# The PEER gate table from one f32r product a token, with GpSimd making the weights' low parts

## The chip, the cores and the metric

The kernel runs on one core of one Trainium2 chip. The metric is the device time of one execution in microseconds (us); the lower, the better. The time before is 3590.15 us, the median of 3 runs (3589.37 to 3594.89).

Engines are named as in the profile: PE (TensorE, with PEld for its weight loads), ACT (ScalarE), DVE (VectorE), POOL (GpSimd), SP (the queue that issues the input DMAs).

## The reference, cut to what matters

The model is two transformer blocks on 512 tokens of width 1024. The part at hand is the PEER layer of the first block. It retrieves, for each token, 8 heads x 16 of 128 x 128 = 16384 single-neuron experts, and sums them with gates:

```python
top_s, pos = lax.top_k(cand, PEER_TOPK)
ids = jnp.take_along_axis(cand_id, pos, axis=-1)      # row * 128 + column
gate = jax.nn.softmax(top_s, axis=-1)
act = jax.nn.gelu(jnp.einsum('ted,td->te', u_emb[ids], xb))
out = jnp.einsum('te,ted->td', gate * act, v_emb[ids])
```

## The kernel before, in words

All matrix products with float32 accuracy are made of float32r parts: a weight tile is split into a high part (a copy rounded to f32r, made by ACT) and a low part (tile minus high part), and three products of 512 columns replace one. The PEER layer (`phase_peer`) computes all 16384 experts for all 512 tokens densely, and multiplies by a gate table that is zero nearly everywhere.

**Hidden units.** For each of 128 row groups n of 128 experts, `hidden` (L457) makes 24 matmuls of 512 columns (8 chunks of the width, three parts each; L463), ACT applies Gelu (`gelu`, L538) and writes the result to DRAM (`spill`, L543). `hi` (L443, ACT) and `lo` (L447) split the weight tile first. The tiles come through a ring of 4 slots, and the two parts lie in 2 slots each, so that `hi(n)` waits for `hidden(n-2)` to be done (semaphore `tiles_used`). The 128 steps are staged as `AHEAD` = 32 (`lo` on POOL, while DVE works out the top-k), `SPREAD` = 64 (the table stage) and `REST` = 32.

**The gate table.** In the table stage each step n also handles two batches m = 2n and 2n+1 of `GT` = 4 tokens. The row, column and gate of a token's 128 chosen experts lie on the 128 partitions (`rowT`, `colT`, `gateT`). A token's 128 x 128 table is the product of two one-hot matrices in float32: `cols` (iota equal to the column) as the weights, and `rows` (iota equal to the row, times the gate) as the moving side. `outers` (L467, matmuls at L477) makes 4 such products a batch into one PSUM bank of the four banks 4 to 7. `evac` (L562, ACT) copies a bank into the table in SBUF, transposed so that a token's entries lie 128 bytes apart, and `save` writes 32 tokens' table to DRAM.

**Who makes the one-hots.** `rows` always by DVE (`hots`, L776, one TENSOR_SCALAR of 128x128 a token). `cols` by POOL for even batches (`offset` L645 subtracts, `equal` L650 compares with 0), by ACT for m % 4 == 1 (`columns`: 4 times Abs at L550, one Relu of 1-x at L553), by DVE for m % 4 == 3 (L779). There are 8 batch buffers (`GR` = 8). `lo` is on DVE.

**What sets the order.** Each engine has its own program, a fixed list with semaphore waits, written by hand. One step of the table stage before:

```python
PE:   hidden(n); outers(2n); outers(2n+1)
ACT:  hi(n+1); gelu(n); spill(n-1); evac(2n); evac(2n+1); columns(2n+9) in every second step
DVE:  hots(2n); hots(2n+1); lo(n+1)
POOL: offset and equal, for the even batches
```

The loops have bodies of 8 steps; a loop's body is compiled once, and ACT's body holds two table loads (`ACT_TABLE_LOAD`), one at its first activation and one at its first Gelu.

After the 128 steps `mix` multiplies the hidden units, weighted by the table, with the second expert matrix. The second block follows. These parts are not touched.

Of the kernel before, what the change touches and what calls it, by code (L numbers as in the profile page):

```python
# [410 lines left out]
def phase_peer(nc, e, nxt, x, wt, val, idx, idxf, k, tb, mb):  # L411
# [9 lines left out]
    hot, hot_pool, hot_act = e.sem("hot"), e.sem("hot_pool"), e.sem("hot_act")  # L421
# [17 lines left out]
    def hi(act, it, step, n):  # L439

        act.wait_ge(e.slot_full[ring(n)], it * (4 * step) + 16 * ((base + n) // SLOTS + 1))
        act.wait_ge(e.tiles_used, it * step + (base + n + 3))
        A_(uh[:, slot(n)], e.ring[:, ring(n), 0:D], ACT.Copy).then_inc(e.hi_done, 1)  # L443

    def lo(eng, ops, it, step, n):
        eng.wait_ge(e.hi_done, it * step + (base + n + 1))
        ops.tensor_tensor(ul[:, slot(n)], e.ring[:, ring(n), 0:D], uh[:, slot(n)].bitcast(F32),  # L447
                          ALU.subtract).then_inc(e.lo_done, 1)

    def sp_program(sp):  # L450
        stream(e, sp, name, nxt)

    def pe_program(pe):
# [12 lines left out]

        def outers(it, m):  # L467

            r = m % GR
            pe.wait_ge(hot, it * 16 + (m + 1))  # L470
            if r % 2 == 0:
                pe.wait_ge(hot_pool, it * 8 + (m // 2 + 1))
            if r % 4 == 1:
                pe.wait_ge(hot_act, it * 4 + (m // 4 + 1))
            pe.wait_ge(stored, it * 16 + (m + 1))
            for t in range(GT):
                mm = M(e.ps[:, 4 + m % 4, t * P:(t + 1) * P], tb.cols[:, r, t], tb.rows[:, r, t])  # L477
            mm.then_inc(outer, 1)

        def mix(it, g, first, last):  # L480

            pe.wait_ge(e.lo_done, it * 8 + (base + NK + g + 1))
            pe.wait_ge(ready, it * 8 + (g + 1))
            for o in order:
                if first and o == 4:

                    pe.wait_ge(stored, batches + 4)
# [39 lines left out]
    def act_program(act):  # L527
        for s in range(SLOTS):
            act.sem_inc(spilled[s], 16)
        for s in range(2):  # L530
            act.sem_inc(saved[s], 16)
        act.sem_inc(stored, 4)
# [22 lines left out]
        def evac(it, m):  # L555

            blk = m // BK
            if m % BK == 0:
                act.wait_ge(saved[blk], it * 16 + 16)
            act.wait_ge(outer, it * 16 + (m + GR + 1))  # L560
            t0 = (m % BK) * GT
            A_(tb.table[:, blk].rearrange("p i t -> p t i")[:, t0:t0 + GT, :],  # L562
               e.ps[:, 4 + m % 4, :].rearrange("p (t i) -> p t i", t=GT), ACT.Copy).then_inc(stored, 1)

        def save(it, blk):

            act.wait_ge(stored, it * 16 + (BK * (blk + 1) + 4))
# [17 lines left out]
        for n in range(nb):  # L585
            act.wait_ge(turned, n + 1)
            for j, y in enumerate((e.rowT, e.colT, e.gateT)):
                cp = A_(y[:, n * P:(n + 1) * P], e.ps[:, 4 + n, j * P:(j + 1) * P], ACT.Copy)
            cp.then_inc(spread, 1)

        act.wait_ge(spread, nb)
        columns(0, 1)
        columns(0, 5)

        def table_step(it, n, more):
            hi(act, it, 8, AHEAD + n + 1)
            gelu(it, 8, AHEAD + n)
            spill(it, 8, AHEAD + n - 1)
            evac(it, 2 * n)
            evac(it, 2 * n + 1)  # L600
            if n % 2 == 0 and more:
                columns(it, 2 * n + 1 + GR)
            if n % 4 == 3:
                save(it, n // 4)

# [1 line left out]
            for n in range(8):  # L607
                table_step(it, n, True)
        for n in range(8):
            table_step(SPREAD // 8 - 1, n, n < 4)  # L610
        with act.Fori(0, REST // 4) as it:
            for n in range(AHEAD + SPREAD, AHEAD + SPREAD + 4):
                hi(act, it, 4, n + 1)
                gelu(it, 4, n)
                spill(it, 4, n - 1)
        spill(0, 4, NK - 1)

        def round_w(it, g):
# [13 lines left out]
    def pool_program(pool):  # L632
# [2 lines left out]
            for n in range(4):  # L635
                lo(pool, nc.gpsimd, it, 4, n)

        def offset(it, j):

            pool.wait_ge(outer, it * GR + (2 * j + 1))  # L640
            if not isinstance(it, int) or j:

                pool.wait_ge(pool_offset, it * (GR // 2) + j)
            col = it * (GR * GT) + 2 * j * GT
            nc.gpsimd.tensor_tensor(tb.cols[:, 2 * j % GR], c["iota"].unsqueeze(1).broadcast_to([P, GT, P]),  # L645
                                    e.colT[:, bass.ds(col, GT)].unsqueeze(2).broadcast_to([P, GT, P]),
                                    ALU.subtract).then_inc(pool_offset, 1)
# [5 lines left out]
        turns = batches // GR  # L653
        pool.wait_ge(spread, nb)
        offset(0, 0)
        with pool.Fori(0, turns - 1) as it:
            for j in range(GR // 2):
                offset(it, j + 1)
                equal(j)
        for j in range(GR // 2 - 1):  # L660
            offset(turns - 1, j + 1)
            equal(j)
        pool.wait_ge(pool_offset, GR // 2 * turns)
        equal(GR // 2 - 1)
# [28 lines left out]
    def dve_program(dve):  # L693
# [75 lines left out]

        def hots(it, m):  # L770

            r = m % GR
            dve.wait_ge(outer, it * 16 + (m + 1))
            for t in range(GT):
                col = it * (16 * GT) + (m * GT + t)
                oh = V.tensor_scalar(tb.rows[:, r, t], c["iota"], e.rowT[:, bass.ds(col, 1)],  # L776
                                     e.gateT[:, bass.ds(col, 1)], ALU.is_equal, ALU.mult)
                if r % 4 == 3:
                    oh = V.tensor_scalar(tb.cols[:, r, t], c["iota"], e.colT[:, bass.ds(col, 1)], None,  # L779
                                         ALU.is_equal)  # L780
            oh.then_inc(hot, 1)

        dve.wait_ge(e.lo_done, base + AHEAD)
        lo(dve, V, 0, 8, AHEAD)
        dve.wait_ge(spread, nb)
        with dve.Fori(0, SPREAD // 8) as it:
            for n in range(8):
                hots(it, 2 * n)
                hots(it, 2 * n + 1)
                lo(dve, V, it, 8, AHEAD + n + 1)  # L790
        with dve.Fori(0, REST // 4) as it:
            for n in range(AHEAD + SPREAD, AHEAD + SPREAD + 4):
                lo(dve, V, it, 4, n + 1)

        def weigh(it, g):
            q = g // GQ
# [1979 lines left out]
def hybrid_kernel(nc, w, out, stop=None):  # L2776
    with ExitStack() as ctx:
# [56 lines left out]
        with ExitStack() as outer:  # L2834
# [41 lines left out]
            tb.rows, tb.cols = a.take(GR, GT, P), a.take(GR, GT, P)  # L2876
# [162 lines left out]
```

## Time and profile before

| | |
|---|---|
| median of 3 runs | 3590.15 us (3589.37 to 3594.89) |
| the profiled execution: own time, span | 3598.26 us, 3596.5 us |
| PE busy, share of the span | 3509.6 us, 98% |
| DVE, ACT, POOL busy | 1772.6, 1283.5, 500.7 us |
| table stage, first to last table matmul | 699.8 to 1164.8 us |
| mean granted clock of TensorE | 0.985 |

The profile comes from one execution; "busy" is the time in which an engine executes instructions, with waits, register work and DMA issue left out. A matmul's duration overlaps that of the next, so that its cost is the distance from start to start. A float32 matmul shows as two records. A start on POOL or ACT just behind its releaser shows how long a semaphore takes. An engine's idle time matters only where that engine is waited for.

### The profile page before, as it was taken

The page shows a single profiled execution, that of the slowest core. Times are in us where ns is not written, and L with a number is a line of the kernel's source. Part 1 is how long each engine was busy: PE and PEld are TensorE (multiplying, and loading weights), DVE is VectorE, ACT ScalarE, POOL GpSimd, SP SyncE. Part 2 cuts the span into 40 slices and gives each one's busy share as a digit, 9 for nine tenths or more (in the row PEclk, how much of TensorE's full clock was granted, in tenths as well). Part 3 has the DMA queues.
Part 4 walks back from the last instruction along what each step waited for, and adds up shares of the span by engine and source line. Part 5 has one row for each costly group of instructions (what it writes and reads, how often), then busy time and mean ns, then how long its engine had stood idle before and what let it go on. Part 6 is the DMA issues. An engine that isn't in the chain of part 4 may idle for free. (4 is left out here: it accounts for less than half of the span.)

```text
span 3596.5 us, 52641 instructions
## 1 busy us (share of the span) xinstructions
PE 3509.6 (98%) x19484; PEld 2990.6 (83%) x19484; DVE 1772.6 (49%) x3403; ACT 1283.5 (36%) x1851; POOL 500.7 (14%) x428
## 2 busy tenths in 40 slices
PE   8999999999999999999999999999999999899999
PEld 8966787788888878888888899998889789768887
DVE  7344599566665224444444543335445456654333
ACT  4244222466665232222222322233223333333232
POOL 0100125433332001111111010010100000111011
PEclk9989999999999999999999999999999989999999
DMA  4200224355555546666666422222222100122221
GB/s 148 77 18 18 88 95 140 123 175 175 178 181 184 190 144 190 194 189 193 190 193 197 129 88 94 82 94 74 91 85 77 59 1 1 36 76 97 93 99 69
DMA packets 115447, 416.05 MB, mean 116 GB/s; under 512 B 14192, under 2 KB 14320, under 8 KB 113008
## 3 DMA queue, kind: packets, MB, share of 16 engines
q1 hardware_dynamic: 75632, 279.93, 23.6%
q0 software_dynamic: 18944, 67.12, 6.4%
q10 hardware_dynamic: 20736, 67.12, 5.0%
q8 instruction: 95, 1.56, 0.2%
q14 instruction: 40, 0.33, 0.0%
HBM read 344.91 MB, written 69.21 MB: 115 GB/s over the span
## 5 line engine op out<-in xcount | busy, mean ns | idle before, releaser
L447 DVE TENSOR_TENSOR w_lo<-ring,w_hi 128x1024 fp32r<-128x1024 f32 x224 | 275.4, 1230 | 698.0 <-ACT w_hi L443 698.0
L183 DVE TENSOR_TENSOR w_lo<-ring,w_hi 128x1024 fp32r<-128x1024 f32 (+2 forms) x157 | 205.9, 1311 | 568.7 <-ACT w_hi L177 568.7
L443 ACT ACTIVATE w_hi<-ring 128x1024 fp32r<-128x1024 f32 x255 | 270.2, 1059 | 505.9 <-PE ps L493 488.8
L463 PE MATMUL ps<-hn_hi,w_hi 128*128 128x512 f32 x1024 | 408.1, 398 | 3.6 <-POOL w_lo L447 1.4
L463 PE MATMUL ps<-hn_lo,w_hi 128*128 128x512 f32 x1024 | 404.5, 395 | 0.0
L463 PE MATMUL ps<-hn_hi,w_lo 128*128 128x512 f32 x1024 | 402.9, 393 | 0.0
L493 PE MATMUL ps<-units_hi,w_hi 128*128 128x512 f32 x1024 | 399.1, 390 | 2.7 <-DVE units_lo L804 2.7
L493 PE MATMUL ps<-units_hi,w_lo 128*128 128x512 f32 x1024 | 399.0, 390 | 0.0
L493 PE MATMUL ps<-units_lo,w_hi 128*128 128x512 f32 x1024 | 398.9, 390 | 0.0
L177 ACT ACTIVATE w_hi<-ring 128x1024 fp32r<-128x1024 f32 (+2 forms) x170 | 190.2, 1119 | 455.0 <-PE ps L241 381.0
L241 PE MATMUL ps<-f_hn_hi,w_hi 128*128 128x264 f32 (+1 forms) x1056 | 284.6, 324 | 8.9 <-DVE f_hn_lo L855 8.5
L241 PE MATMUL ps<-f_hn_lo,w_hi 128*128 128x264 f32 (+1 forms) x1056 | 284.9, 324 | 0.0
L241 PE MATMUL ps<-f_hn_hi,w_lo 128*128 128x264 f32 (+1 forms) x1056 | 283.7, 323 | 0.0
L463 PEld LDWEIGHTS ps<-hn_hi,w_hi 128*128 128x128 f32 x1024 | 192.8, 188 | 48.8 <-ACT scratch L538 4.2
L463 PEld LDWEIGHTS ps<-hn_hi,w_lo 128*128 128x128 f32 x1024 | 192.6, 188 | 43.5
L493 PEld LDWEIGHTS ps<-units_hi,w_hi 128*128 128x128 f32 x1024 | 192.6, 188 | 43.1 <-issue 3.1
L463 PEld LDWEIGHTS ps<-hn_lo,w_hi 128*128 128x128 f32 x1024 | 192.5, 188 | 42.1
L493 PEld LDWEIGHTS ps<-units_lo,w_hi 128*128 128x128 f32 x1024 | 192.6, 188 | 40.1
L493 PEld LDWEIGHTS ps<-units_hi,w_lo 128*128 128x128 f32 x1024 | 192.5, 188 | 40.1
L241 PE MATMUL ps<-hn_hi,mix_w_hi 128*128 128x264 f32 (+1 forms) x752 | 211.8, 332 | 6.0 <-DVE hn_lo L855 4.1
L538 ACT ACTIVATE scratch<-ps 128x512 f32<-128x512 f32 x128 | 76.6, 598 | 375.7 <-PE ps L463 375.6
L241 PE MATMUL ps<-hn_lo,mix_w_hi 128*128 128x264 f32 (+1 forms) x752 | 209.6, 329 | 0.0
(432 smaller groups left out, 6723.6 us busy)
## 6 DMA issues: line engine op xcount, KB each, us to landing
ring<-in_w_uv SPq DMA_DIRECT2D x256, 512.0 KB, 3.4
ring<-in_f_up SPq DMA_DIRECT2D x88, 512.0 KB, 3.2
expert_units<-scratch ACTq DMA_DIRECT2D x128, 256.0 KB, 2.6
gate_table<-peer ACTq DMA_DIRECT2D x16, 2048.0 KB, 7.2
peer<-gate_table POOLq DMA_DIRECT2D x32, 1024.0 KB, 8.0
peer<-expert_units POOLq DMA_DIRECT2D x128, 256.0 KB, 3.7
ring<-in_w_in SPq DMA_DIRECT2D x29, 512.0 KB, 3.3
ring<-in_w_late SPq DMA_DIRECT2D x25, 512.0 KB, 3.3
```

The lines of the kernel that those rows point to most:

```text
L177: self.nc.scalar.activation(self.h[:, self.slot(k), 0:self.cols], e.ring[:, self.ring(k), 0:self.cols], ACT.Copy).then_inc(e.hi_done, 1)
L183: self.nc.vector.tensor_tensor(self.l[:, self.slot(k), 0:self.cols], e.ring[:, self.ring(k), 0:self.cols], self.h[:, self.slot(k), 0:self. ...
L241: mm = nc.tensor.matmul(e.ps[:, bank + hf, 0:tokens.width], lhsT[:, wt.slot(k), col], rhs(part, c)[:, cut], start=(c == 0 and j == 0), sto ...
L443: A_(uh[:, slot(n)], e.ring[:, ring(n), 0:D], ACT.Copy).then_inc(e.hi_done, 1)
L447: ops.tensor_tensor(ul[:, slot(n)], e.ring[:, ring(n), 0:D], uh[:, slot(n)].bitcast(F32), ALU.subtract).then_inc(e.lo_done, 1)
L463: mm = M(e.ps[:, n % 2, :], u[:, slot(n), ch * P:(ch + 1) * P], x[part][:, ch, META:L], start=(ch == 0 and j == 0), stop=(ch == DC - 1 and ...
L493: mm = M(e.ps[:, o, :], v[:, slot(NK + g), col], w[:, g % 2], start=(first and j == 0), stop=(last and j == 2))
L538: A_(units[:, n % SLOTS, 0:T], e.ps[:, n % 2, :], ACT.Gelu).then_inc(gelu_done, 1)
```

## The change

- **PE** (`outers`): one float32r matmul a token with 256 columns takes the place of the float32 matmul with 128 columns. The moving side `rows` holds the high part of the gate and the low part beside it ([2, 128] a token); a batch takes two PSUM banks, and two batches are in flight (`stored` starts at 2) where four were.
- **ACT**: `evac` goes; `high` (L558) copies the high half of a batch from PSUM to SBUF. `columns` now makes all the one-hot columns: for every batch one Abs (L551) and one Relu (L553) over 512 elements, in place, on differences that POOL made. `hi` is made two steps ahead and comes after `gelu`.
- **DVE**: `hots` makes a token's rows by one SCALAR_TENSOR_TENSOR of 128x256 (L773); `evac` (L787) adds the low half in PSUM to the copied high half and writes the table. `lo` leaves DVE in the table stage.
- **POOL** (`table_step`): `lo`, then two `offset` (L643); `equal` goes.

The core of the diff:

```diff
@@ PE @@
         def outers(it, m):
-            r = m % GR
             pe.wait_ge(hot, it * 16 + (m + 1))
-            if r % 2 == 0:
-                pe.wait_ge(hot_pool, it * 8 + (m // 2 + 1))
-            if r % 4 == 1:
-                pe.wait_ge(hot_act, it * 4 + (m // 4 + 1))
+            pe.wait_ge(hot_col, it * 16 + (m + 1))
             pe.wait_ge(stored, it * 16 + (m + 1))
             for t in range(GT):
-                mm = M(e.ps[:, 4 + m % 4, t * P:(t + 1) * P], tb.cols[:, r, t], tb.rows[:, r, t])
+                mm = M(both(m)[:, t].rearrange("p x i -> p (x i)"), tb.cols[:, m % GR, t],
+                       tb.rows[:, m % 4, t].rearrange("p x i -> p (x i)"))
@@ ACT @@
         def columns(it, m):
-            act.wait_ge(outer, it * 16 + (m + 1))
-            for t in range(GT):
-                col = it * (16 * GT) + (m * GT + t)
-                off = A_(tb.cols[:, m % GR, t], c["iota"], ACT.Abs, bias=e.colT[:, bass.ds(col, 1)], scale=-1.0)
-            off.then_inc(act_offset, 1)
-            act.wait_ge(act_offset, it * 4 + (m // 4 + 1))
-            A_(tb.cols[:, m % GR], tb.cols[:, m % GR], ACT.Relu, bias=e.one, scale=-1.0).then_inc(hot_act, 1)
+            x = tb.cols[:, m % GR]
+            act.wait_ge(pool_offset, it * 16 + (m + 1))
+            A_(x, x.bitcast(F32), ACT.Abs).then_inc(act_offset, 1)
+            act.wait_ge(act_offset, it * 16 + (m + 1))
+            A_(x, x.bitcast(F32), ACT.Relu, bias=e.one, scale=-1.0).then_inc(hot_col, 1)
+        def high(it, m):
+            act.wait_ge(outer, it * 16 + (m + GR + 1))
+            A_(tb.high[m % 2], both(m)[:, :, 0], ACT.Copy).then_inc(copied, 1)
         def table_step(it, n, more):
-            hi(act, it, 8, AHEAD + n + 1)
+            if more:
+                columns(it, 2 * n + 4)
+                columns(it, 2 * n + 5)
             gelu(it, 8, AHEAD + n)
             spill(it, 8, AHEAD + n - 1)
-            evac(it, 2 * n)
-            evac(it, 2 * n + 1)
-            if n % 2 == 0 and more:
-                columns(it, 2 * n + 1 + GR)
+            hi(act, it, 8, AHEAD + n + 2)
+            high(it, 2 * n)
+            high(it, 2 * n + 1)
             if n % 4 == 3:
                 save(it, n // 4)
@@ POOL @@
+        def offset(it, m):
+            pool.wait_ge(outer, it * 16 + (m + 1))
+            nc.gpsimd.tensor_tensor(tb.cols[:, m % GR], c["iota"].unsqueeze(1).broadcast_to([P, GT, P]),
+                                    e.colT[:, bass.ds(it * (16 * GT) + m * GT, GT)].unsqueeze(2).broadcast_to([P, GT, P]),
                                     ALU.subtract).then_inc(pool_offset, 1)
-        def equal(j):
-            nc.gpsimd.tensor_scalar(tb.cols[:, 2 * j], tb.cols[:, 2 * j], 0.0, None,
-                                    ALU.is_equal).then_inc(hot_pool, 1)
+        def table_step(it, n, more):
+            lo(pool, nc.gpsimd, it, 8, AHEAD + n + 2)
+            if more:
+                offset(it, 2 * n + 6)
+                offset(it, 2 * n + 7)
         pool.wait_ge(spread, nb)
+        for m in range(6):
+            offset(0, m)
@@ DVE @@
         def hots(it, m):
-            dve.wait_ge(outer, it * 16 + (m + 1))
+            dve.wait_ge(outer, it * 16 + (m + GR - 4 + 1))
             for t in range(GT):
                 col = it * (16 * GT) + (m * GT + t)
-                oh = V.tensor_scalar(tb.rows[:, r, t], c["iota"], e.rowT[:, bass.ds(col, 1)],
-                                     e.gateT[:, bass.ds(col, 1)], ALU.is_equal, ALU.mult)
+                parts = tb.gates[:, bass.ds(col, 1)].bitcast(F32).rearrange("p o x -> p (o x)")
+                oh = V.scalar_tensor_tensor(out=tb.rows[:, m % 4, t],
+                                            in0=c["iota"].unsqueeze(1).broadcast_to([P, 2, P]),
+                                            scalar=e.rowT[:, bass.ds(col, 1)],
+                                            in1=parts.unsqueeze(2).broadcast_to([P, 2, P]),
+                                            op0=ALU.is_equal, op1=ALU.mult)
+        def evac(it, m):
+            dve.wait_ge(copied, it * 16 + (m + 1))
+            V.tensor_tensor(tb.table[:, blk].rearrange("p i t -> p t i")[:, t0:t0 + GT, :], tb.high[m % 2],
+                            both(m)[:, :, 1], ALU.add).then_inc(stored, 1)
+        def table_step(it, n, more):
+            if more:
+                hots(it, 2 * n + 2)
+                hots(it, 2 * n + 3)
+            evac(it, 2 * n)
+            evac(it, 2 * n + 1)
```

ACT, one step in the body of the table loop. `scratch<-ps` is Gelu's result, `peer` the region of one-hots and table. Before:

```order
L443 ACTIVATE w_hi<-ring 128x1024 [waits tiles_used,slot_full3]
L536 REGISTER_ALU
L538 ACTIVATE scratch<-ps 128x512 [waits spilled1,tiles_used]
L542 REGISTER_ALU
L543 ISA [waits gelu_done]
L543 DMA expert_units<-scratch 128x512
L560 REGISTER_ALU
L562 ACTIVATE peer<-ps 128x4x128 [waits outer]
```

With the change, from the first of a step's two `columns` (the same two rows again, and a second `high`, are left out):

```order
L551 ACTIVATE hot_cols<-hot_cols 128x512 [waits pool_offset]
L553 ACTIVATE hot_cols<-hot_cols,misc 128x512 [waits act_offset]
...
L540 ACTIVATE scratch<-ps 128x512 [waits spilled3,tiles_used]
...
L444 ACTIVATE w_hi<-ring 128x1024 [waits tiles_used,slot_full2]
L557 REGISTER_ALU
L558 ACTIVATE scratch<-ps 128x512 [waits outer]
```

The copy to `w_hi` stood ahead of Gelu and now stands behind it, and two pairs of activations that wait for POOL (`pool_offset`) stand ahead of Gelu.

POOL in the body of its table loop, before:

```order
L643 REGISTER_ALU [waits outer]
L645 ISA [waits pool_offset]
L645 TENSOR_TENSOR peer<-const_tab,turned 128x512
L650 TENSOR_SCALAR peer<-peer 128x512
L640 REGISTER_ALU
```

With the change, one step:

```order
L448 TENSOR_TENSOR w_lo<-ring,w_hi 128x1024 [waits hi_done]
L642 REGISTER_ALU
L643 ISA [waits outer]
L643 TENSOR_TENSOR hot_cols<-const_tab,turned 128x512
L642 REGISTER_ALU
L643 ISA [waits outer]
L643 TENSOR_TENSOR hot_cols<-const_tab,turned 128x512
```

The comparison is gone, the subtraction is there twice a step where it was there once, and the weights' low part, which waits for ACT's `hi_done`, stands ahead of both.

## Rows read from the trace of the kernel before

**Rows 1.** The page: span, and busy time of each engine.

```profile
span 3596.5 us, 52641 instructions
PE 3509.6 (98%) x19484; PEld 2990.6 (83%) x19484; DVE 1772.6 (49%) x3403; ACT 1283.5 (36%) x1851; POOL 500.7 (14%) x428
```

**Rows 2.** Windows, inside the table stage: busy of each engine, granted clock, DMA.

```profile
720.00:1135.00 415.00, 415.00 (x2265) 355.82 (x2264) 257.39 (x623) 267.80 (x380) 141.87 (x113) 1.00 0.51 177
```

**Rows 3.** Timeline of PE (start, duration), one table step; L477's records.

```profile
761.13 0.48 PE L463 MATMUL ps<-hn_hi,w_hi 128*128 128x512 f32 x1
...
766.77 1.95 PE L477 MATMUL ps<-peer 128*128 128x128 f32 x16
768.47 0.48 PE L463 MATMUL ps<-hn_hi,w_hi 128*128 128x512 f32 x1
...
L477 PE MATMUL ps<-peer x1024: 272/275/275, 699.8 to 1164.8; 128*128 128x128 f32 x171
```

**Rows 4.** Timeline of PE, float32r matmuls of 264 columns, full rate.

```profile
2100.12 0.41 PE L241 MATMUL ps<-f_hn_lo,w_hi 128*128 128x264 f32 x2
...
2109.68 0.41 PE L241 MATMUL ps<-f_hn_lo,w_hi 128*128 128x264 f32 x2
```

**Rows 5.** Timeline of ACT: Relu and its follower, Gelu and its follower; L562 min/median/max.

```profile
823.34 0.72 ACT L553 ACTIVATE peer<-peer,misc 128x512 f32<-128x512 f32 x1
823.97 1.04 ACT L443 ACTIVATE w_hi<-ring 128x1024 fp32r<-128x1024 f32 x1
...
1170.74 0.60 ACT L538 ACTIVATE scratch<-ps 128x512 f32<-128x512 f32 x1 [2.78 <-PE ps L463]
1171.43 1.06 ACT L443 ACTIVATE w_hi<-ring 128x1024 fp32r<-128x1024 f32 x1
...
L562 ACT ACTIVATE peer<-ps x128: 1082/1130/1226, 702.0 to 1165.1; 128x512 f32<-128x512 f32 x128
```

**Rows 6.** From ACT's high part to POOL's low part; POOL's durations at both lines.

```profile
648.53 1.06 ACT L443 ACTIVATE w_hi<-ring 128x1024 fp32r<-128x1024 f32 x1
...
649.67 3.13 POOL L447 TENSOR_TENSOR w_lo<-ring,w_hi 128x1024 fp32r<-128x1024 f32 x1 [3.48 <-ACT w_hi L443]
...
L447 POOL TENSOR_TENSOR w_lo<-ring,w_hi x32: 2384/2408/4379, 497.6 to 677.5; 128x1024 fp32r<-128x1024 f32 x32
...
L645 POOL TENSOR_TENSOR peer<-const_tab,turned x64: 1032/1044/1187, 693.9 to 1134.9; 128x512 f32<-128x512 f32 x64
```

**Rows 7.** Timeline of DVE and POOL where their two-input instructions meet.

```profile
534.24 2.29 DVE L752 TENSOR_TENSOR peer<-peer,const_tab 128x2048 f32<-128x2048 f32 x1
536.45 4.49 DVE L753 TENSOR_TENSOR peer<-peer,const_tab 128x2048 f32<-128x2048 f32 x1
...
534.77 4.01 POOL L447 TENSOR_TENSOR w_lo<-ring,w_hi 128x1024 fp32r<-128x1024 f32 x1 [3.31 <-ACT w_hi L443]
```

**Rows 8.** DVE: three kinds of instruction near the new ones.

```profile
532.65 0.29 DVE L741 SCALAR_TENSOR_TENSOR peer<-peer 128x128 f32<-128x128 f32 x1
532.86 0.28 DVE L743 TENSOR_TENSOR peer<-peer 128x128 f32<-128x128 f32 x1
...
L1507 DVE SCALAR_TENSOR_TENSOR scratch<-z,param_tab,scratch x12: 767/768/770, 2717.5 to 2793.6; 128x527 f32<-128x527 f32 x12
...
L1157 DVE TENSOR_TENSOR scratch<-ps,scratch x44: 681/696/708, 2070.7 to 3526.4; 128x528 f32<-128x528 f32 x22, 128x512 f32<-128x512 f32 x22
```

**Rows 9.** ACT's table loads at L443 and L538.

```profile
L443 ACT ACT_TABLE_LOAD x7: 1283/1283/1283, 697.8 to 1049.9; - x7
...
L538 ACT ACT_TABLE_LOAD x8: 1283/1283/1283, 504.0 to 1053.3; - x8
```

**Rows 10.** PE's gap, and windows (PE, PEld, DVE, ACT, POOL busy, PEclk, DMA).

```profile
2878.92 0.71 PE L2586 MATMUL ps<-gates,const_tab 16*128 16x128 f32 x4 [2.10 <-DVE delta L2675]
...
2880.00:2884.00 4.00, 2.81 (x16) 2.44 (x15) 1.54 (x6) 1.10 (x3) 0.00 (x0) 0.50 0.01 2
...
510.00:680.00 170.00, 167.33 (x719) 134.48 (x718) 142.96 (x392) 49.50 (x60) 85.08 (x30) 1.00 0.40 134
```

More of the change, by code:

```diff
@@ L420, in phase_peer @@
     expd, gated, turned, spread = (e.sem(n) for n in ("gates_exp", "gated", "gates_turned", "gates_spread"))
-    hot, hot_pool, hot_act = e.sem("hot"), e.sem("hot_pool"), e.sem("hot_act")
+    hot, hot_col = e.sem("hot"), e.sem("hot_col")
+    parted, copied = e.sem("gate_parts"), e.sem("high_copied")
     pool_offset, act_offset = e.sem("pool_offset"), e.sem("act_offset")
@@ L448, in lo, with both @@
                           ALU.subtract).then_inc(e.lo_done, 1)
+    def both(m):
+        at = (4 + 2 * (m % 2)) * WIDE
+        return e.psf[:, at:at + 2 * WIDE].rearrange("p (t x i) -> p t x i", t=GT, x=2)
     def sp_program(sp):
@@ L485, in mix @@
                 if first and o == 4:
-                    pe.wait_ge(stored, batches + 4)
+                    pe.wait_ge(stored, batches + 2)
                 if first and o == 0:
@@ L545, in columns @@
         def columns(it, m):
-            act.wait_ge(outer, it * 16 + (m + 1))
-            for t in range(GT):
-                col = it * (16 * GT) + (m * GT + t)
-                off = A_(tb.cols[:, m % GR, t], c["iota"], ACT.Abs, bias=e.colT[:, bass.ds(col, 1)], scale=-1.0)
-            off.then_inc(act_offset, 1)
-            act.wait_ge(act_offset, it * 4 + (m // 4 + 1))
-            A_(tb.cols[:, m % GR], tb.cols[:, m % GR], ACT.Relu, bias=e.one, scale=-1.0).then_inc(hot_act, 1)
[L555 to L559, printed above, removed]
+            x = tb.cols[:, m % GR]
[4 more added lines that the diff above has]
+        def high(it, m):
             act.wait_ge(outer, it * 16 + (m + GR + 1))
-            t0 = (m % BK) * GT
-            A_(tb.table[:, blk].rearrange("p i t -> p t i")[:, t0:t0 + GT, :],
-               e.ps[:, 4 + m % 4, :].rearrange("p (t i) -> p t i", t=GT), ACT.Copy).then_inc(stored, 1)
+            A_(tb.high[m % 2], both(m)[:, :, 0], ACT.Copy).then_inc(copied, 1)
         def save(it, blk):
-            act.wait_ge(stored, it * 16 + (BK * (blk + 1) + 4))
+            act.wait_ge(stored, it * 16 + (BK * (blk + 1) + 2))
             act.dma_start(e.gtab[it * 2 + blk],
@@ L587, in act_program @@
             for j, y in enumerate((e.rowT, e.colT, e.gateT)):
-                cp = A_(y[:, n * P:(n + 1) * P], e.ps[:, 4 + n, j * P:(j + 1) * P], ACT.Copy)
-            cp.then_inc(spread, 1)
+                A_(y[:, n * P:(n + 1) * P], e.ps[:, 4 + n, j * P:(j + 1) * P], ACT.Copy)
+            A_(tb.gates[:, n * P:(n + 1) * P, 0], e.ps[:, 4 + n, 2 * P:3 * P], ACT.Copy).then_inc(spread, 1)
         act.wait_ge(spread, nb)
-        columns(0, 1)
-        columns(0, 5)
+        hi(act, 0, 8, AHEAD + 1)
+        for m in range(4):
+            columns(0, m)
         def table_step(it, n, more):
-            hi(act, it, 8, AHEAD + n + 1)
+            if more:
+                columns(it, 2 * n + 4)
+                columns(it, 2 * n + 5)
             gelu(it, 8, AHEAD + n)
             spill(it, 8, AHEAD + n - 1)
-            evac(it, 2 * n)
-            evac(it, 2 * n + 1)
-            if n % 2 == 0 and more:
-                columns(it, 2 * n + 1 + GR)
+            hi(act, it, 8, AHEAD + n + 2)
+            high(it, 2 * n)
+            high(it, 2 * n + 1)
             if n % 4 == 3:
@@ L609, in act_program @@
         for n in range(8):
-            table_step(SPREAD // 8 - 1, n, n < 4)
-        with act.Fori(0, REST // 4) as it:
+            table_step(SPREAD // 8 - 1, n, n < 6)
+        with act.Fori(0, REST // 4 - 1) as it:
             for n in range(AHEAD + SPREAD, AHEAD + SPREAD + 4):
-                hi(act, it, 4, n + 1)
                 gelu(it, 4, n)
+                hi(act, it, 4, n + 2)
                 spill(it, 4, n - 1)
+        for n in range(NK - 4, NK):
+            gelu(0, 4, n)
+            if n < NK - 1:
+                hi(act, 0, 4, n + 2)
+            spill(0, 4, n - 1)
         spill(0, 4, NK - 1)
@@ L636, in pool_program @@
                 lo(pool, nc.gpsimd, it, 4, n)
[L638 to L646, printed above, removed]
-                                    ALU.subtract).then_inc(pool_offset, 1)
-        def equal(j):
-            nc.gpsimd.tensor_scalar(tb.cols[:, 2 * j], tb.cols[:, 2 * j], 0.0, None,
-                                    ALU.is_equal).then_inc(hot_pool, 1)
-        turns = batches // GR
-        pool.wait_ge(spread, nb)
[L655 to L664, printed above, removed]
+        def offset(it, m):
+            pool.wait_ge(outer, it * 16 + (m + 1))
+            nc.gpsimd.tensor_tensor(tb.cols[:, m % GR], c["iota"].unsqueeze(1).broadcast_to([P, GT, P]),
+                                    e.colT[:, bass.ds(it * (16 * GT) + m * GT, GT)].unsqueeze(2).broadcast_to([P, GT, P]),
+                                    ALU.subtract).then_inc(pool_offset, 1)
+        def table_step(it, n, more):
[3 more added lines that the diff above has]
+                offset(it, 2 * n + 7)
+        pool.wait_ge(spread, nb)
+        for m in range(6):
+            offset(0, m)
+        pool.wait_ge(e.lo_done, base + AHEAD + 2)
+        with pool.Fori(0, SPREAD // 8 - 1) as it:
+            for n in range(8):
+                table_step(it, n, True)
+        for n in range(8):
+            table_step(SPREAD // 8 - 1, n, n < 5)
         def load_gates(it, q):
@@ L783, in dve_program @@
         dve.wait_ge(e.lo_done, base + AHEAD)
         lo(dve, V, 0, 8, AHEAD)
+        lo(dve, V, 0, 8, AHEAD + 1)
+        dve.sem_inc(stored, 2)
         dve.wait_ge(spread, nb)
-        with dve.Fori(0, SPREAD // 8) as it:
-            for n in range(8):
[L788 to L791, printed above, removed]
+        V.tensor_tensor(tb.gates[:, :, 1], e.gateT, tb.gates[:, :, 0].bitcast(F32), ALU.subtract).then_inc(parted, 1)
@@ L792, in dve_program @@
+        dve.wait_ge(parted, 1)
+        hots(0, 0)
+        hots(0, 1)
+        with dve.Fori(0, SPREAD // 8 - 1) as it:
+            for n in range(8):
+                table_step(it, n, True)
+        for n in range(8):
+            table_step(SPREAD // 8 - 1, n, n < 7)
+        dve.wait_ge(e.lo_done, base + AHEAD + SPREAD + 2)
+        with dve.Fori(0, REST // 4 - 1) as it:
             for n in range(AHEAD + SPREAD, AHEAD + SPREAD + 4):
-                lo(dve, V, it, 4, n + 1)
+                lo(dve, V, it, 4, n + 2)
@@ L795, in weigh @@
+        for n in range(NK - 4, NK - 1):
+            lo(dve, V, 0, 4, n + 2)
         def weigh(it, g):
@@ L2875, in hybrid_kernel @@
             a, tb = Arena(region), Env()
-            tb.rows, tb.cols = a.take(GR, GT, P), a.take(GR, GT, P)
+            a.take(2 * GR * GT * P)
+            tb.rows = work.at("hot_rows", 0, GR // 2, GT, 2, P, dt=F32R)
+            tb.cols = work.at("hot_cols", 4 * GR * GT * P, GR, GT, P, dt=F32R)
+            tb.gates = work.at("gate_parts", room + 12 * T, T, 2, dt=F32R)
+            tb.high = [x[:, 0:GT * P].rearrange("p (t i) -> p t i", t=GT) for x in (e.r0, e.r1)]
             tb.table = a.take(2, NK, GB)
```

9 lines of the change are left out of this document (4 added, 5 removed).

## The prediction

> **What bounds the kernel now.** I read the page first: PE is busy for 3509.6 of 3596.5 us [rows 1], so time is won or lost only where PE's own work shrinks or where PE is made to wait. Then the windows: between 720 and 1135 us, deep in the table stage, PE is busy for all of the 415 us at full clock, while DVE works for 257, ACT for 268 and POOL for 142 us [rows 2]. So nobody holds PE there today. Then the timeline of PE for one step: 24 matmuls of 512 columns take from 761.13 to 766.77, which is 5.64 us, and the eight float32 table matmuls (16 records) from 766.77 to 768.47, 1.70 us, so a step takes 7.34 us [rows 3]. L477's first and last record, 699.8 and 1164.8, are 63 steps and 15 records of about 0.11 us apart, which gives 7.355 us a step on average [rows 3]. The stage has 64 steps. The AHEAD, REST and mix stages and the second block keep PE's work as it is.
>
> **What the change takes from PE.** A token's product becomes one float32r matmul of 256 columns. The nearest row is the 264-column float32r matmul with a weight load of its own: from 2100.12 to 2109.68 there are 13 rounds of six, 78 matmuls in 9.56 us, 0.123 us each [rows 4]. Eight take 0.98 us where 1.70 were. PE alone would then need 5.64 + 0.98 = 6.62 us a step, and 64 x 0.72 = 46 us would be won. It cannot be much more (256 columns are 3% fewer than 264) and not less than nothing (1.70 us, if 256 columns cost as much as the two float32 records).
>
> **What the change puts on the other engines.** The costs per step, with their rows:
> - ACT: the high part (start to start of what follows on POOL) 1.14 us [rows 6]; Gelu to its follower 0.69 us [rows 5]; Abs and Relu of 512 elements four times. Relu today takes 0.63 us to its follower [rows 5]; the new Abs has the same shape, and each Relu waits for the Abs before it by a semaphore, so I take 0.65 for all four, 2.60 us. Two `high` copies have Gelu's shape and source, 0.60 each; the 1.13 us of the scattered copy at L562 [rows 5] leave ACT. Together 5.6 us.
> - POOL: the low part 2.41 us when undisturbed, and two subtractions of 1.04 us each [rows 6], 4.49 us.
> - DVE: eight SCALAR_TENSOR_TENSOR of 256 elements. The same kind takes 0.29 us for 128 elements and 0.768 for 527 [rows 8], a slope of 1.2 ns, so 0.44 us for 256; start to start is 0.08 less (532.65 to 532.86 for a duration of 0.29 [rows 8]), and register pointers give some back: 0.40 us, eight times 3.2 us. The `evac` add with one operand from PSUM took 0.70 us for 512 to 528 elements written densely [rows 8]; its bounds are that and 1.23, since the scattered write cost ACT 0.53 us more than a dense one (1.13 against 0.60 [rows 5]). I take 1.2, as the same scatter is written; two are 2.4 us. Together 5.6 us.
>
> The Trainium skill warns, in "Vector Engine (DVE) Microarchitecture Reference", points that are easy to get wrong, that this instruction halves its throughput with two float32 inputs in SBUF. The row speaks against it (527 elements in 768 ns, two inputs in SBUF [rows 8]); by the rule a token's rows would cost 0.67 us and eight of them 5.4, and the sum would go up by what the access rival below has.
>
> Every engine alone fits into 6.62 us. But the fixed lists tie two of them into a **ring**. ACT makes hi(n+2) behind gelu(n); POOL's lo(n+2) waits for it; POOL makes offset(2n+6) and offset(2n+7) behind lo(n+2), in its own order; ACT's columns(2n+6) and columns(2n+7) wait for them, and they stand *ahead* of gelu(n+1) and so of hi(n+3), for which lo(n+3) waits. The stock of six offsets and four columns made before the loop is consumed without any step of slack, since the offsets that step n+1 needs are made in step n behind lo(n+2). One turn of the ring is one step:
>
> hi to POOL's start 1.14 + lo 2.41 + first offset 1.04 + signal to ACT 0.08 + two columns 2.60 + Gelu 0.69 = 7.96 us.
>
> The signal is from the same row pair (1.14 less 1.06 [rows 6]). The way round by the second offset is shorter: 1.14 + 2.41 + 2.08 + 0.08 + 1.30 + 0.69 = 7.70 us. The two `high` copies (1.20 us) lie beside lo and the first offset (3.45 us) and cost nothing; if they came late (an `outers` kept back by DVE), the ring would wait by as much. So the ring is longer than PE's 6.62, and longer than the 7.355 of now.
>
> **The shared access of DVE and POOL** comes on top. POOL's low part at 534.77 took 4.01 us instead of 2.41: it met DVE's L752, ran out only once that had ended at 536.5, and then L753, the same kind as L752, took 4.49 instead of 2.29 because it stood until POOL had ended at 538.8 [rows 7]. One instruction with two inputs in SBUF keeps out the other engine's for its whole length. A step now holds POOL's 4.49 and DVE's 3.2 us of such work, 7.7 us of a turn of 8. Bounds for what this adds to the ring: nothing, if DVE's eight fall into the stretch in which ACT has the ring (columns, Gelu, hi: 4.4 us); 0.40 for each of lo and the first offset, 0.8 us, if each meets a running DVE instruction. DVE's adds wait for `high`, which comes just behind the start of lo, so its eight mostly fall behind POOL's work; I take 0.14. A step then takes 8.10 us.
>
> **Table loads.** ACT's loop body has two loads of 1.28 us [rows 9], at its first activation and its first Gelu, once in 8 steps. Now PE covers them. In the ring they stand behind the wait for POOL and ahead of hi: 8 x 2 x 1.28 = 20 us (none to 20; for each to be hidden the ring must be waiting for another engine at that moment).
>
> **Entry of the stage.** ACT makes hi(33) and four columns ahead of its first Gelu, POOL makes six offsets ahead of lo(34), and DVE's rows share the access with these. PE's first table matmuls could start some us later than 699.8: 0 to 5 us, taken at 2. The `save` of every fourth step now waits for DVE's adds (2.4 us behind the first `high`, within the 3.45 us for which ACT waits for POOL anyway): nothing. REST: the low part is made earlier than now and PE does the same matmuls; nothing.
>
> **Sum.** 64 x (8.10 - 7.355) = 48, + 20 + 2 = +70 us. The profiled execution took 3598.26 us, so it would take 3668; the median shown lies 8 us lower, so 3660 us.
>
> **The rivals.**
> - *PE stays the bound* (the other side). If the ring turned in less than 6.62 us, the step would be PE's: -46 us, 3544 us. It decides at a turn of 7.355 us: below it the change wins. It needs 1.3 us less than the sum of measured durations, for instance if Abs and Relu on 512 elements took 0.3 us each. Rows 5 and 6 speak against it. Chance 0.11. A turn within 0.1 us of 7.355, no change, 0.03.
> - *The access becomes the bound.* If DVE's 3.9 us (0.49 each, with 0.05 more for the pointers than its duration) and POOL's 4.49 exclude each other and the adds (2.4) fall between them instead of beside POOL, a turn is up to 10.8 us; with partial overlap 9 to 10: 64 x 1.65 to 64 x 2.65 and the loads, +126 to +190 us, 3716 to 3780 us. For it speaks how little is free (0.4 us of 8.1); against it that ACT's share of the ring leaves DVE 4.4 us. Chance 0.13. In the Trainium skill, "SBUF — State Buffer", SBUF: two separate sides, only DVE instructions with two SBUF inputs or in a two-port mode take the shared pair, by which the adds, with one input in PSUM, would stay beside POOL; no row here shows it.
> - *PE's clock.* PE would idle 8.1 - 6.6 = 1.5 us a step, more at the loads. After a gap of 2.10 us at 2878.92 the granted clock was 0.50 for the next stretch, while 170 us with 2.7 us of gaps in all kept 1.00 [rows 10]. If each step's gap cost 4 us at half clock, 2 us of PE work are lost, PE needs 8.6 and with its gap 9 or more: +105 us and up, 3695 us. The gaps are shorter than the one that did it; chance 0.08.
> - *The change doesn't do what it says*: 256-column products as dear as before. PE would need 7.34, still below the ring: the result would be the forecast's. That is why the ring, not the product, decides.
>
> **The numbers.** The forecast's case has 0.65, with a range of its own from 3626 (ring at 7.75 by 0.2 us of overlap, half of the loads hidden) to 3700. The range to 8 in 10 goes from 3615 to 3745; it leaves out the faster and same cases (0.14) and the top of the access case. About 0.2% (7 us) is what a measurement of this kernel can tell from no change. Faster 0.11, same 0.03, slower 0.86.
>
> **What would show it.** Right: between PE's table matmuls and its next 512-column matmul a gap of about 1.5 us, ended by POOL's w_lo; ACT idle before Abs, ended by POOL; POOL idle before w_lo, ended by ACT; steps of 8 to 8.5 us; 256-column matmuls at 0.12 us. Wrong: PE busy all of the stage with steps of 6.6 us; or DVE without idle time; or the gaps ended by the one-hot rows or by the adds; or a granted clock well below 1.

## The result, and the profile after

The changed kernel takes 3631.51 us, the median of 4 runs (3630.99 to 3634.01), against 3592.22 us before (4 runs). The ratio is 1.0107 with a 95% interval of 1.0093 to 1.0121: **39 us slower**. The forecast was 3660 us, slower, with a range of 3615 to 3745. The direction was right and the time lies in the range, but 70 us were forecast where 39 came.

The page of the changed kernel, as [rows 1]:

```profile
span 3632.3 us, 51347 instructions
PE 3488.7 (96%) x18972; PEld 2943.7 (81%) x18972; DVE 1911.6 (53%) x3340; ACT 1315.6 (36%) x1951; POOL 642.8 (18%) x492
```

Windows over the same stretch of the table stage (busy of PE, PEld, DVE, ACT and POOL, granted clock, DMA), as [rows 2]:

```profile
720.00:1135.00 415.00, 366.90 (x1649) 289.47 (x1649) 343.94 (x515) 272.87 (x423) 245.64 (x156) 0.97 0.45 164
```

PE is no longer busy all of the time: 48 of 415 us are lost. Its products' line says what PE waited for there, as [rows 3] (durations min/median/max in ns, first and last start; then idle us and times; the idle lines also count the products' weight loads on PEld, to which `issue` belongs, and PE by itself waited for L787 for 55.1 us and for L773 for 1.9):

```profile
L479 PE MATMUL ps<-hot_rows,hot_cols x512: 276/283/554, 697.4 to 1202.4; 128*128 128x256 f32 x171
...
  issue: 87.5, 110
  DVE peer L787: 55.1, 103
  DVE hot_rows L773: 4.4, 4
```

From the first to the last product it takes 505.0 us, where it took 465.0 [rows 3]: +40.0 us. From PE's first matmul of the layer to the first product it is 2.9 us longer. Together that is a little more than the difference of the medians. (In the profiled executions the changed kernel was 5.3 us shorter before the layer and 1.8 us shorter behind the last product, where both kernels do the same, so that the spans are only 35.8 us apart. All comparisons of the stage below go from the first to the last product.)

One turn of the ring in the changed kernel, from the timelines of ACT, POOL and DVE (start, duration, idle before and what ended it):

```profile
804.84 1.05 ACT L444 ACTIVATE w_hi<-ring 128x1024 fp32r<-128x1024 f32 x1
805.79 1.07 ACT L558 ACTIVATE scratch<-ps 128x512 f32<-128x512 f32 x2
809.68 0.63 ACT L551 ACTIVATE hot_cols<-hot_cols 128x512 fp32r<-128x512 f32 x1 [2.82 <-POOL hot_cols L643]
810.34 0.72 ACT L553 ACTIVATE hot_cols<-hot_cols,misc 128x512 fp32r<-128x512 f32 x1
810.97 0.61 ACT L551 ACTIVATE hot_cols<-hot_cols 128x512 fp32r<-128x512 f32 x1
811.62 0.72 ACT L553 ACTIVATE hot_cols<-hot_cols,misc 128x512 fp32r<-128x512 f32 x1
812.25 0.58 ACT L540 ACTIVATE scratch<-ps 128x512 f32<-128x512 f32 x1
812.73 1.05 ACT L444 ACTIVATE w_hi<-ring 128x1024 fp32r<-128x1024 f32 x1
...
805.97 2.40 POOL L448 TENSOR_TENSOR w_lo<-ring,w_hi 128x1024 fp32r<-128x1024 f32 x1 [3.03 <-ACT w_hi L444]
808.33 2.49 POOL L643 TENSOR_TENSOR hot_cols<-const_tab,turned 128x512 fp32r<-128x512 f32 x2
...
806.41 2.03 DVE L787 TENSOR_TENSOR peer<-scratch,ps 128x512 f32<-128x512 f32 x2 [0.81 <-ACT scratch L558]
808.29 4.80 DVE L773 SCALAR_TENSOR_TENSOR hot_rows<-const_tab,turned,gate_parts 128x256 fp32r<-128x256 f32 x8
```

There is no idle time in it that one of the two engines does not owe to the other: hi 804.84, 1.13 to the low part at 805.97, 2.36 to the subtraction at 808.33, 1.35 to Abs at 809.68, 2.57 for the two columns, 0.48 from Gelu at 812.25 to the next hi at 812.73. The turn is 7.89 us. DVE's eight rows, which start with POOL's subtractions, take 4.80 us.

Where the body of ACT's loop ends and begins, the turn has the two table loads in it:

```profile
820.58 1.04 ACT L444 ACTIVATE w_hi<-ring 128x1024 fp32r<-128x1024 f32 x1
...
825.10 1.28 ACT L551 ACT_TABLE_LOAD   x1 [2.50 <-DVE peer L787]
...
829.08 1.28 ACT L540 ACT_TABLE_LOAD   x1
...
830.86 1.05 ACT L444 ACTIVATE w_hi<-ring 128x1024 fp32r<-128x1024 f32 x1
```

This one is 10.28 us. A body of 8 steps takes 64.8 us by the starts of `hi` (7.6 to 7.9 for seven steps, 10.3 for one) where it took 58.7.

### The profile page after: what moved, and what is told of

The parts are those of the page before. It is cut to its first block and busy times, and to the rows that moved or that the text cites. A ratio compares the mean times of both kernels' runs of the same rounds, so it can differ in the third digit from the quotient of the medians.

```text
span 3632.3 us, 51347 instructions
## 1 busy us (share of the span) xinstructions
PE 3488.7 (96%) x18972; PEld 2943.7 (81%) x18972; DVE 1911.6 (53%) x3340; ACT 1315.6 (36%) x1951; POOL 642.8 (18%) x492
## 5 line engine op out<-in xcount | busy, mean ns | idle before, releaser
L448 DVE TENSOR_TENSOR w_lo<-ring,w_hi 128x1024 fp32r<-128x1024 f32 x160 | 197.0, 1231 | 518.5 <-ACT w_hi L444 518.5
L448 POOL TENSOR_TENSOR w_lo<-ring,w_hi 128x1024 fp32r<-128x1024 f32 x96 | 243.2, 2534 | 393.6 <-ACT w_hi L444 303.3
L773 DVE SCALAR_TENSOR_TENSOR hot_rows<-const_tab,turned,gate_parts 128x256 fp32r<-128x256 f32 x512 | 308.1, 669 | 0.0
```

What stands on the lines that cost most here:

```text
L773: oh = V.scalar_tensor_tensor(out=tb.rows[:, m % 4, t], in0=c["iota"].unsqueeze(1).broadcast_to([P, 2, P]), scalar=e.rowT[:, bass.ds(col, 1)],
```

## The experiments

All edits are to the changed kernel. The stage column is the time from the first to the last product in each run's trace (before 465.0, changed kernel 505.0).

| run | median us | ratio to before, 95% | stage us |
|---|---|---|---|
| e1_pool_order | 3636.55 | 1.0127 (1.0101 to 1.0154) | 507.2 |
| e2_act_order | 3630.05 | 1.0108 (1.0085 to 1.0131) | 498.1 |
| e3_half_rows | 3632.89 | 1.0114 (1.0093 to 1.0135) | 505.3 |
| e4_twice_products | 3627.60 | 1.0092 (1.0073 to 1.0112) | 502.2 |
| e5_flat_act | 3625.04 | 1.0078 (1.0054 to 1.0103) | 491.2 |
| e6_pool_order_half_rows | 3555.12 | 0.9896 (0.9879 to 0.9913) | 427.8 |
| e7_gates_in_psum | 3624.86 | 1.0092 (1.0075 to 1.0108) | 496.2 |
| e8_psum_act_order | 3541.26 | 0.9856 (0.9839 to 0.9872) | 412.3 |
| e9_psum_pool_order | 3552.15 | 0.9890 (0.9873 to 0.9906) | 422.4 |
| e10_psum_both_orders | 3542.47 | 0.9856 (0.9834 to 0.9879) | 412.4 |
| e11_e8_twice_products | 3601.47 | 1.0025 (1.0012 to 1.0038) | 473.3 |

### Opening the ring: e1 and e2

```diff
@@ POOL, table_step @@
-            lo(pool, nc.gpsimd, it, 8, AHEAD + n + 2)
             if more:
                 offset(it, 2 * n + 6)
                 offset(it, 2 * n + 7)
+            lo(pool, nc.gpsimd, it, 8, AHEAD + n + 2)
```

> GpSimd's two subtractions of a step stand ahead of its low part instead of behind it; nothing else changes. The ring theory (ACT's hi, POOL's lo, POOL's offset, ACT's columns, Gelu, hi, one turn a step, 7.85 us by the changed kernel's profile): the columns no longer wait for lo, one turn now serves two steps, and the step falls to what comes next, PE's 6.6 or DVE's 6.9 us, 3560 to 3580 us. The access theory (POOL's 4.5 and DVE's 3.2 us of two-input instructions exclude each other, 7.7 us a step): the step stays at 7.6 to 7.8 us, 3610 to 3632 us. The buffer theory (PE waits for the adds because only two batches fit into PSUM): no change, 3631 us.

```diff
@@ ACT, table_step @@
-            if more:
-                columns(it, 2 * n + 4)
-                columns(it, 2 * n + 5)
             gelu(it, 8, AHEAD + n)
             spill(it, 8, AHEAD + n - 1)
             hi(act, it, 8, AHEAD + n + 2)
             high(it, 2 * n)
             high(it, 2 * n + 1)
+            if more:
+                columns(it, 2 * n + 4)
+                columns(it, 2 * n + 5)
```

> ACT makes the columns of batches 2n+4 and 2n+5 at the end of step n, behind the two high copies, instead of at its start, ahead of Gelu; nothing else changes. Ring theory: the differences that a step needs are then a whole step old, the ring is open as in e1_pool_order, 3560 to 3580 us. Access theory: as in e1, 3610 to 3632 us. Buffer theory: no change.

Neither won anything that the intervals show: 3636.55 and 3630.05 us. e2 falls into the range of the access theory; e1 lies above every range that was given. Taken by themselves the two times speak against the ring. But the ring is open in both: between 720 and 1135 us ACT waited for POOL's subtractions for 124.5 us in the changed kernel, and not once in e1 or e2. And the steps are not those of the changed kernel. By the starts of `hi`, e1's body from 769.4 us has steps of 4.97, 5.73, 11.18, 7.63, 5.47, 6.44, 10.61 and 11.28 us, no longer seven equal ones. Windows of e1 and of e2 (columns as above):

```profile
720.00:1135.00 415.00, 366.72 (x1630) 295.86 (x1629) 384.72 (x508) 275.74 (x420) 250.36 (x153) 0.93 0.45 162
```

```profile
720.00:1135.00 415.00, 373.75 (x1671) 301.72 (x1670) 410.74 (x527) 276.63 (x423) 264.68 (x157) 0.94 0.44 164
```

DVE is now busy for 385 and 411 of 415 us, with the same work as before. The timeline of e2 shows with what (DVE first, then POOL):

```profile
767.91 8.64 DVE L773 SCALAR_TENSOR_TENSOR hot_rows<-const_tab,turned,gate_parts 128x256 fp32r<-128x256 f32 x8
...
786.16 3.22 DVE L773 SCALAR_TENSOR_TENSOR hot_rows<-const_tab,turned,gate_parts 128x256 fp32r<-128x256 f32 x8
```

```profile
768.17 2.40 POOL L643 TENSOR_TENSOR hot_cols<-const_tab,turned 128x512 fp32r<-128x512 f32 x2
770.92 2.59 POOL L448 TENSOR_TENSOR w_lo<-ring,w_hi 128x1024 fp32r<-128x1024 f32 x1 [0.35 <-ACT w_hi L444]
773.48 2.40 POOL L643 TENSOR_TENSOR hot_cols<-const_tab,turned 128x512 fp32r<-128x512 f32 x2
```

The eight rows take 3.22 us where POOL does not hold them up and 8.64 us where POOL works nearly without a break: DVE stands for POOL's instructions, and "busy" counts that. So the ring was opened, and the shared access of DVE and POOL took its place at about the same length. In part this is still an inference here, since PE's granted clock fell too (0.93 and 0.94), and ACT's Gelu waits for PE in both runs (57 and 80 us of the window). As an estimate from these rows, the clock can explain at most 0.07 x 415 = 29 us and 0.06 x 415 = 25 us of the window. e7 and e8 below take away the access itself.

### Less work for one engine: e3 and e4

```diff
@@ DVE, hots @@
-            for t in range(GT):
+            for t in range(GT // 2):
@@ PE, outers @@
-                       tb.rows[:, m % 4, t].rearrange("p x i -> p (x i)"))
+                       tb.rows[:, m % 4, t % 2].rearrange("p x i -> p (x i)"))
```

> Leaves out DVE's rows of every batch's third and fourth token; their products use the rows of the first two. DVE does 1.6 us less a step, all of it on the access shared with POOL. Ring theory: POOL's offset loses only its 0.14 us of waiting, so 64 x 0.1 to 0.2 us, 3618 to 3626 us. Access theory: 7.7 less 1.6 is under PE's 6.6, so the step is PE's: 3555 to 3570 us.

It took 3632.89 us with a stage of 505.3: the 1.6 us a step that DVE no longer works are worth nothing. DVE is busy for 263.59 us of the window instead of 343.94, and POOL's subtractions are as long as before (1224 ns on average against 1225). This is the mirror of e1 and e2: with the access relieved, the ring holds the step alone. The gain of 0.1 to 0.2 us a step that was expected did not come, since the four rows that are left of a step's eight still meet POOL's subtractions.

```diff
@@ PE, outers @@
-            for t in range(GT):
+            for t in [t for t in range(GT) for _ in range(2)]:
```

> Each of the table's products is computed twice in a row (same result); PE does 8 matmuls of about 0.12 us more a step, 0.98 us. Ring theory: PE idles 1.1 us a step, and the copies wait for the products for 0.5 us more a batch, for which ACT has time while POOL works: 0 to 15 us more, 3631 to 3646 us. Were PE, or the way products, copy, add, products the bound: 63 us more, 3694 us.

It took 3627.60 us, 502.2 for the stage: PE's additional work is free in the changed kernel. The time is even 3 us below the range that was expected. In this run more of the steps last 7.6 us instead of 7.9, and POOL's subtractions take 1180 ns on average instead of 1225; why they meet DVE less was not tested.

### Both at once: e6

e6 has the edits of e1 and of e3.

> e1_pool_order and e3_half_rows together: the subtractions ahead of the low part, and the rows of every batch's third and fourth token left out. Each alone changed nothing. Two bounds in parallel (the ring at 7.85 us and the shared access at 7.7 to 8.0 us a step, each hiding the other): with both gone the step is PE's 6.5 to 6.6 us, 64 x 1.3 us less, 3540 to 3560 us. Another bound (PSUM's two batches, the copies, the adds): no change, 3615 to 3635 us.

It took 3555.12 us, 76 us less than the changed kernel, although each edit alone gave nothing. Two bounds of nearly the same length lay side by side, and each hid the other. That the second one is the access, and not DVE's own amount of work, is not shown by this pair, which takes both away; e7 to e9 leave DVE all of its work.

### What the two engines share: e7

```diff
@@ DVE @@
-                parts = tb.gates[:, bass.ds(col, 1)].bitcast(F32).rearrange("p o x -> p (o x)")
+                parts = e.psf[:, bass.ds(2 * WIDE + 2 * col, 2)]
...
         dve.wait_ge(parted, 1)
+        V.tensor_copy(e.psf[:, 2 * WIDE:4 * WIDE],
+                      tb.gates.bitcast(F32).rearrange("p t x -> p (t x)")).then_inc(parted, 1)
+        dve.wait_ge(parted, 2)
```

> DVE's rows read the gates' two parts from PSUM (banks 2 and 3, free in this stage, filled once by a copy of 1024 columns) instead of SBUF; all is computed. If what shuts DVE and POOL out of one another is two inputs in SBUF, a step's eight rows take 3.3 us instead of 4.8, and POOL's subtractions 1.04 instead of 1.2. The ring still turns in 7.7: 3615 to 3628 us. If DVE's rows still meet POOL: no change in either.

Groups of instructions between 715 and 1120 us, the changed kernel first, then e7 (count, then busy us and mean ns of one):

```profile
L773 DVE SCALAR_TENSOR_TENSOR hot_rows<-const_tab,turned,gate_parts 128x256 fp32r<-128x256 f32 x403 | 243.1, 671 | 0.0
L643 POOL TENSOR_TENSOR hot_cols<-const_tab,turned 128x512 fp32r<-128x512 f32 x101 | 121.9, 1225 | 0.0
```

```profile
L773 DVE SCALAR_TENSOR_TENSOR hot_rows<-const_tab,turned,ps 128x256 fp32r<-128x256 f32 x411 | 164.4, 477 | 0.0
L643 POOL TENSOR_TENSOR hot_cols<-const_tab,turned 128x512 fp32r<-128x512 f32 x103 | 105.3, 1045 | 0.0
```

With one of the two inputs in PSUM the rows no longer wait for POOL: 477 ns instead of 671, and POOL's subtraction is back at 1045 [rows 6]. What kept the two apart is thus shown to be DVE's pair of SBUF inputs. The stage is 8.8 us shorter (496.2; median 3624.86, 7 us less): every turn of the ring is now 7.6 us, but for the one in 8 with the table loads (10.3).

### Both at once, with all of the work: e8, e9, e10

e8 has the edits of e7 and e2, e9 those of e7 and e1, e10 all three.

> e7_gates_in_psum and e2_act_order together, all computed: the ring open and the shared access free. Two bounds in parallel: PE's 6.5 to 6.6 us a step, table loads covered by PE, 3545 to 3565 us, below the kernel before. If only the ring or only the access counted, one of e2 and e7 would have shown it alone: then 3615 to 3630 us here too.

> e7_gates_in_psum and e1_pool_order together, all computed: the same two bounds taken away, the ring by the other engine's order. ACT's columns still stand ahead of Gelu, whose wait for PE then sets them late: 3545 to 3575 us by the theory of two parallel bounds; else 3615 to 3635 us.

> e8_psum_act_order with GpSimd's subtractions ahead of its low part as well. If the ring was open already in e8, the low part now comes 2 us later and nothing is won: 3540 to 3550 us.

e8 takes 3541.26 us, ratio 0.9856: 51 us *below* the kernel before, 90 below the changed kernel. It computes everything that they do. The time is 4 us below the range that was expected. Its window, and PE's timeline at a step's end:

```profile
720.00:1135.00 415.00, 415.00 (x2026) 347.36 (x2025) 313.01 (x598) 317.48 (x491) 267.76 (x183) 1.00 0.58 206
```

```profile
853.86 0.39 PE L469 MATMUL ps<-hn_hi,w_lo 128*128 128x512 f32 x1
854.09 1.11 PE L479 MATMUL ps<-hot_rows,hot_cols 128*128 128x256 f32 x8
855.03 0.40 PE L469 MATMUL ps<-hn_hi,w_hi 128*128 128x512 f32 x1
```

PE is busy for all of the window at full clock (the table stage ends inside it, at 1109). Eight products take 0.94 us from start to start of their neighbours, and a step 6.51 us. e9 has 10.39 us for one step in 8, where the columns with their table load stand ahead of Gelu and a `save` waits for DVE's adds; e8 has the columns at the step's end, and that step is 7.7 us, followed by one of 5.4. By the starts of `hi`, a body takes 53.6 us in e9 and 52.1 in e8, which over six bodies is 9 of the 10 us between the two. e10 adds nothing to e8, as expected.

### The product's price: e11, and the table loads: e5

> e8_psum_act_order with each table product computed twice (same result), 8 matmuls of 0.12 us more a step. PE being the bound of e8, 64 x 0.92 to 0.98 us more: 3600 to 3604 us; in the changed kernel the same edit cost nothing (e4). It gives the price of a product where PE is the bound.

e11 (e8 with e4's edit) takes 60.2 us more than e8, 61.0 in the stage: 0.95 us a step. The same edit cost the changed kernel nothing. So a float32r product costs what PE's timeline says, once PE is the bound.

```diff
@@ ACT @@
-        with act.Fori(0, SPREAD // 8 - 1) as it:
+        for it in range(SPREAD // 8 - 1):
```

> The changed kernel with ACT's table loop written out (7 bodies of 8 steps without a loop), so that the two table loads and the branch of each body go; the order of everything is kept. Ring theory: the long steps of 10.3 us become 7.85, 7 x 2.4 = 17 us less, 3612 to 3617 us; if the shared access is as tight a bound as the ring, it gives part of that back, 3615 to 3628 us. Loads hidden: 3631 us.

The stage fell by 13.8 us, to 491.2. A body of 8 steps takes 62.6 us instead of 64.8, with no step above 7.9. The median fell by 6 us only, and its four runs lie between 3617.91 and 3628.24; in the profiled one, 7 of the 13.8 us are lost again behind the layer, where the kernels do the same. I take the stage's number for the loads; where the 7 us went stays open.

## Why the prediction was right or wrong

**Right: the other side's argument.** PE alone would have won 46 us. e8 won 51 against before, and e11 priced the eight products at 0.95 us, where the 264-column row [rows 4] gave 0.98.

**Right: the ring.** Its place, its members and its direction were those of the trace: ACT idle before Abs until POOL, POOL idle before the low part until ACT. e3 shows it alone at work: with the access relieved, the steps stayed at 7.6 to 7.9 us. e7's steps of 7.6 us are the ring in which DVE and POOL no longer hold each other up; the prediction's sum for that, 7.96, was 0.35 too long. The term most to blame is "Gelu to its follower 0.69", 0.21 of the 0.35, read where ACT had to wait for its next input [rows 5]; in the chain, with nothing to wait for, hi starts 0.48 us behind Gelu's start. The rest comes from instructions that overlap by some hundredths at each join (2.36 to POOL's next instead of 2.41, 2.57 for the columns instead of 2.60).

**The waits for the access**, taken at 0.14 us a turn, were 0.2 on average (7.79 us for the turns without loads, against 7.61 in e7): in a disturbed step the subtraction took 1.35 us to Abs (809.68 less 808.33), by the sum 1.12. Not every step is disturbed, which gives the mix of 7.6 and 7.9.

**Mis-sized: the table loads.** Six of the stage's turns between first and last product hold them, at 10.28 less 7.85 = 2.43 us each, 15 us (e5 shows 13.8), not 20: I counted eight bodies, but the first one's loads fall into the entry and the last eight steps have no loop. The last three steps also make no subtractions. **The entry** was +2.9 us against the 2 taken. So the sum: 40 us in the stage instead of 68, of which the step's length accounts for 64 x 0.3 = 19, the loads for 6, the last steps for about 3.

**Wrong: "that is why the ring, not the product, decides".** It decides, but not alone. The rival "the access becomes the bound" was given 0.13 and priced at 9 to 10.8 us a step. In e1 and e2, where the ring was open, a step took 8.1 and 7.9 us on average (507.2 and 498.1 us over 63 steps). The table loads and PE's lower clock are in these averages, so that they bound the access from above; the 7.7 that the prediction had itself added up (POOL's 4.49 and DVE's 3.2), and then set aside as "what this adds to the ring", lies just below. The adds did not fall between as that rival had them: two took 2.03 us from 806.41 on while the low part ran its 2.40 from 805.97. A reader who had trusted the forecast and opened the ring would have gained nothing. The step that failed, though the number held, is to have treated the shared access as a surcharge on the ring, and not as a second ring of its own, of length 7.7, to be compared with 7.96.

**Wrong: how it would show.** I wrote that PE's gap would stand ahead of its 512-column matmuls and be ended by POOL's low part, and that gaps ended by the adds would speak against me. They were ended by the adds (L787, 55.1 us, 103 times): `high` stands behind hi in ACT's list, so the ring holds back the copies and the adds, and with two batches in PSUM the products are the first thing of PE's that notices. PE's releaser named the last link, not the cause. That the two batches are no bound of their own is shown by e8, which keeps them and has PE without a gap. The steps of 8 to 8.5 us did not come either (7.6 to 7.9). ACT's and POOL's waits for each other and the products at 0.12 us came as said.

**The other rivals.** The clock: 0.97 in the window instead of 1.00. In the changed kernel it fell only in the turns with table loads: PE's gap there was 3.05 to 3.09 us, and from 834 to 836 us, just behind the one that ended at 833.62, the granted clock was 0.50 (1.2 GHz). No other gap of PE in the window reached 1.5 us, and away from these turns the clock was 1.00 in every stretch of 8 us. Neither ACT nor DVE nor POOL waited for PE in this window, so the slower PE cost nothing there. In e1 and e2 (0.93 and 0.94), where ACT does wait for PE, it can have cost up to the 29 and 25 us estimated above; its share was not measured. The warning of the Trainium skill ("Vector Engine (DVE) Microarchitecture Reference", points that are easy to get wrong) that SCALAR_TENSOR_TENSOR halves its throughput with two float32 inputs in SBUF does not hold for this instruction: eight took 3.22 us in e2 where POOL did not hold them up, 0.40 each, as from [rows 8], and 3.16 to 3.20 in e7 and e8 with one input in PSUM. The Trainium skill says in "SBUF — State Buffer", Who interferes with whom, that a DVE instruction with at most one SBUF input, outside the two-port modes, does not contend with GpSimd. e7 agrees: 477 against 671 ns.

## What to carry to other kernels

Where engines wait for each other in fixed lists, write down every closed way round one step (here hi, low part, subtraction, columns, Gelu) and every resource that two engines hold in turn, as loops with a length each, and compare them all with the engine that is to be the bound. Two that lie close together hide each other: that an edit removes one of them and gains nothing does not prove that it was no bound. Only the pair of edits tells. Moving the two columns behind the step's copies, and one small operand of DVE's into free PSUM banks, turned +39 us into -51.

## What the runs showed of the hardware that I had not expected

- The price of DVE and POOL meeting is not shared out evenly. In e2 the eight rows took 8.64 us between 767.91 and 776.55, 5.4 more than alone, while POOL's five instructions took 2.40 (two), 2.59 and 2.40 us (two) where alone they take 2.05, 2.41 and 2.05, 0.9 us more together. It can also be POOL that waits: in the same run its low part at 788.26, which began while the eight rows were under way (786.16 to 789.38, undisturbed at 3.22 us), took 3.42 us instead of 2.41, and one at 757.38 took 3.92 beside rows that took 3.23. In these two places POOL began in the middle of DVE's rows; in the meeting of 8.64 us, POOL was already at work when they came.

```profile
757.38 3.92 POOL L448 TENSOR_TENSOR w_lo<-ring,w_hi 128x1024 fp32r<-128x1024 f32 x1 [5.67 <-ACT w_hi L444]
...
788.26 3.42 POOL L448 TENSOR_TENSOR w_lo<-ring,w_hi 128x1024 fp32r<-128x1024 f32 x1 [6.17 <-ACT w_hi L444]
```

- A DVE add with a scattered destination (128 bytes apart, 512 elements, one input in PSUM) took 1081 ns on average in the changed kernel and 1149 in e8, against 0.70 us for the dense one [rows 8] and my 1.2.
